# Sparse layer in another order, and wider products in the state-space mixer

## The reference

```python
h = rmsnorm(x, norm_mix_g)
proj = h @ w_in            # queries, shared key and value, index queries/key/weights, GLU pair
# index: relu(q_i . k_i) over 4 index heads, weighted and summed; causal; the top 128 keys of
#        each query are kept
# a_out: 8 heads of 64 attend over the kept keys (one key and value for all heads)
# b_out: u = a * sigmoid(g); causal depthwise convolution of 31 taps over 512 channels;
#        layer norm over the channels; silu
x = x + concatenate([a_out, b_out], -1) @ w_out
m = rmsnorm(mem, norm_mem_g)           # 256 memory tokens
kc, vc = m @ w_k_cross, m @ w_v_cross  # used by the cross attention that follows
...
# second block, first layer: a diagonal state-space mixer (S5) with complex states
lam_bar = exp(lam * dt); states = scan(lam_bar, B u); y = real(C states) + d * u
```

## Time and profile before

| | us |
|---|---|
| median of 3 runs | 2253.62 |
| lowest, highest | 2250.33, 2256.12 |
| the profiled execution, its own time | 2251.87 |
| its span (first to last instruction) | 2250.0 |
| TensorE busy in it | 2064.4 |
| VectorE busy | 1101.8 |
| ScalarE busy | 734.1 |
| GpSimd busy | 1066.6 |

### The profile page before, as it was taken

One profiled execution on the slowest core, in us unless ns is written; L12 is line 12 of the kernel. 1 busy time (PEld: TensorE's weight loads), 2 busy tenths in 40 slices (PEclk: granted clock), 3 DMA queues, 4 the chain that ended last, 5 costly groups with the idle time before them and its releaser, 6 DMA issues.

```text
span 2250.0 us, 30832 instructions
## 1 busy us (share of the span) xinstructions
PE 2064.4 (92%) x10090; PEld 1660.1 (74%) x10090; DVE 1101.8 (49%) x1843; ACT 734.1 (33%) x1216; POOL 1066.6 (47%) x607
## 2 busy tenths in 40 slices
PE   6879998978999989956899999999999999999997
PEld 5647766866787878735678888888877778888886
DVE  4798663255668676668534122132126743232232
ACT  4213054342322222435343222233224533222223
POOL 4455613633674744761255444456445515444442
PEclk9989987998999999988899999999998989999999
DMA  4314100313233333200133333334320003333332
GB/s 134 85 33 116 34 1 29 103 23 80 76 95 92 98 89 94 75 10 1 47 93 87 101 95 92 103 93 98 99 78 1 0 19 103 103 94 94 103 94 85
DMA packets 330830, 165.76 MB, mean 74 GB/s; under 512 B 21902, under 2 KB 329478, under 8 KB 330758
## 3 DMA queue, kind: packets, MB, share of 16 engines
q1 hardware_dynamic: 330016, 164.17, 25.9%
q10 hardware_dynamic: 742, 0.68, 0.2%
HBM read 162.48 MB, written 2.10 MB: 73 GB/s over the span
## 4 chain that ended last, share of the span: by engine, by line
PE 59%; issue 13%; DVE 8%; POOL 8%; POOLq 5%; DVEq 4%; ACT 2%; DMA 1%; SPq 0%; ACTq 0%
PE ACC L1248 16%; PE ACC L1254 16%; PE ACC L1249 16%; POOL WL L949 6%; POOLq L959 1%; PE O L1345 1%; PE ACC L1379 1%; PE O L1346 1%; PE O L1347 1%; POOLq L1098 1%; PE FOUR L1345 1%; POOLq L1086 1%; DVE CV L1777 1%; DVEq L1781 1%; DVEq L1847 1%
## 5 line engine op out<-in xcount | busy, mean ns | idle before, releaser
L949 POOL TENSOR_TENSOR WL<-RAW,WH 128x1024 fp32r<-128x1024 f32 x300 | 726.9, 2425 | 856.9 <-ACT WH L487 777.5
L1248 PE MATMUL ACC<-PH,WH 128*128 128x512 f32 x1248 | 495.7, 397 | 23.8 <-DVE DS L1787 11.1
L1249 PE MATMUL ACC<-PL,WH 128*128 128x512 f32 x1248 | 491.5, 394 | 0.0
L487 ACT ACTIVATE WH<-RAW 128x1024 fp32r<-128x1024 f32 x300 | 315.8, 1054 | 510.9 <-PE ACC L1254 461.1
L1248 PE MATMUL ACC<-QH,WH 128*128 128x512 f32 (+1 forms) x1136 | 433.6, 386 | 23.8 <-ACT WH L487 14.9
L1249 PE MATMUL ACC<-QL,WH 128*128 128x512 f32 (+1 forms) x1136 | 429.4, 382 | 0.0
L1254 PE MATMUL ACC<-PH,WL 128*128 128x512 f32 x1248 | 310.3, 391 | 0.0
L1248 PEld LDWEIGHTS ACC<-PH,WH 128*128 128x128 f32 x1248 | 238.2, 191 | 81.6 <-DVE DS L1787 12.4
L1254 PE MATMUL ACC<-QH,WL 128*128 128x512 f32 (+1 forms) x1136 | 269.7, 379 | 6.3 <-POOL WL L949 6.0
L1249 PEld LDWEIGHTS ACC<-PL,WH 128*128 128x128 f32 x1248 | 238.0, 191 | 48.9
L1248 PEld LDWEIGHTS ACC<-QH,WH 128*128 128x128 f32 x1136 | 218.0, 192 | 74.8 <-issue 15.9
(11 more groups left out here) (416 smaller groups left out, 2577.6 us busy)
## 6 DMA issues: line engine op xcount, KB each, us to landing
RAW<-in_mlp_w_dram SPq DMA_DIRECT2D x128, 512.0 KB, 3.8
RAW<-in_w_gate_dram SPq DMA_DIRECT2D x22, 512.0 KB, 3.7
RAW<-in_w_up_dram SPq DMA_DIRECT2D x22, 512.0 KB, 3.8
RAW<-in_w_in_dram SPq DMA_DIRECT2D x16, 512.0 KB, 3.8
RAW<-in_w_down_dram SPq DMA_DIRECT2D x16, 512.0 KB, 3.7
RAW<-in_ssm_w_glu_dram SPq DMA_DIRECT2D x16, 512.0 KB, 3.8
RAW<-in_w_kvf_dram SPq DMA_DIRECT2D x16, 512.0 KB, 4.0
RAW<-in_w_k_cross_dram SPq DMA_DIRECT2D x8, 512.0 KB, 3.7
```

The costliest lines, as they stand in the source:

```text
L487: act.activation(WH[:, s], RAW[:, s], ACT.Copy).then_inc(w_hi, 1)
L949: pool.tensor_tensor(WL[:, s], RAW[:, s], WH[:, s], ALU.subtract).then_inc(w_lo, 1)
L1248: pe.matmul(ACC[s][:, 0:n], WH[:, s, k, :], xh[:, k, :], start=(k == 0), stop=False)
L1249: pe.matmul(ACC[s][:, 0:n], WH[:, s, k, :], xl[:, k, :], start=False, stop=False)
```

## The change

The order of the sparse layer becomes: in (with rotations and index products between and inside its units), glu (with the memory's transposes; the rounds of the top 128 run beside it), memk, memv, then the sparse attention with the convolution among its tiles, then out in two halves. The rounds of the top 128 are written out, with other work of VectorE behind the first eleven. Taps 0 to 7 of VectorE come after them, one pair of the others behind each of 23 tiles. TensorE does three diagonal taps before the transposes of the tiles 0 to 10 and 12 to 22 (the last of each run fewer). The first two sets of diagonals are made between memk and memv, six in the attention. Out is split: outa multiplies the attention's half (four chunks of weights, 12 products), outb the branch's half; the layer norm and silu lie beside outa. At the start only the gain of the first norm is awaited ahead of x, and the broadcast of the scales of a norm stands inside unit 1. In the mixer a rotation is two products over 1024 columns and two sums of 512.

```diff
-ORDER = [("glu", 8), ("in", 8), ("memk", 8), ("memv", 8), ("out", 8), ("qc", 8), ("oc", 8)]
+ORDER = [("in", 8), ("glu", 8), ("memk", 8), ("memv", 8), ("outa", 8), ("outb", 8), ("qc", 8), ("oc", 8)]
...
         @block.scalar
+            rounded(5)
+            related(0)
+            rounded(6)
+            related(2)
+            related(4)
+            rounded(7)
...
+            memory(0)
+            gate(0)
+            rounded(11)
+            memory(2)
+            rounded(12)
+            memory(4)
+            gate(1)
+            rounded(13)
...
+            for j in range(8):
+                u = START["outa"] + j
+                round_weights(u + 1, 1 - j % 2, BCH)
+                if j == 2:
+                    standard_deviation("ln")
+                if j == 4:
+                    silu_branch()
...
         @block.gpsimd
+            with pool.Fori(0, 4) as i:
+                for s in range(2):
+                    remainder(START["memk"] + 2 * i + s, s)
+            diagonals(0)
+            diagonals(1)
+            with pool.Fori(0, 4) as i:
+                for s in range(2):
+                    remainder(START["memv"] + 2 * i + s, s)
+            remainder(START["outa"], 0, KC)
+            for j in range(2):
+                pool.wait_ge(u_hi, j + 1)
+                pool.tensor_tensor(UL[:, j, :], U[:, 2 + j, :], UH[:, j, :], ALU.subtract).then_inc(u_lo, 1)
...
         @block.tensor
+            unit(5, 1, PH, PL, between=lambda: relate(2))
+            rotate(4)
+            relate(4)
+            unit(6, 0, PH, PL, between=lambda: relate(6))
...
+            for j in range(1, 8):
+                unit(START["glu"] + j, j % 2, PH, PL)
+                if j < 5:
+                    memory(2 * j - 2)
...
+            def attend_sparse():
+                for t in range(3):
+                    scores("sparse", 0, 0, t)
+                for c in range(4):
+                    b = c % 2
+                    for t in range(8):
+                        n = 8 * c + t
+                        if t + 3 < 8:
+                            scores("sparse", c, b, t + 3)
+                        elif c < 3:
+                            scores("sparse", c + 1, 1 - b, t - 5)
+                        convolve_beside(n)
+                        turn("sparse", c, t)
+                        if t == 0 and c:
+                            values("sparse", c - 1, 1 - b, 1)
+                        if t == TB:
+                            values("sparse", c, b, 0)
+                        if n == CONV_END[1] + 3:
+                            branch_mean()
...
         @block.vector
+            for r in range(TOPK // 8):
                 for b in range(3):
                     dve.max(M8[:, b, :], SC[:, b, 0:(b + 2) * P])
                 dve.drain()
                 for b in range(3):
                     dve.match_replace(SC[:, b, 0:(b + 2) * P], M8[:, b, :], SC[:, b, 0:(b + 2) * P], TAKEN)
+                if r == 0:
+                    projected(7)
+                    roped(4)
+                    sines(5)
...
+                elif r == 3:
+                    roped(7)
+                    glu(0)
+                    glu_value(1)
+                    memory(0)
+                elif r == 4:
+                    glu_gate(1)
+                    memory(2)
...
+                        if n + 8 < CONVW:
+                            taps(n + 8, n + 9)
...
+            def turned(x, cos, sin, n):
+                both = [P, 2, 4, n]
+                dve.tensor_tensor(RTC[:, :, :, 0:n], x, cos[:, None].to_broadcast(both), ALU.mult)
+                return dve.tensor_tensor(RTS[:, :, :, 0:n], x, sin[:, None].to_broadcast(both), ALU.mult)
```

More of the change, by code:

```diff
@@ L46 @@
 TAKEN = -3.0e38
+CONV_END = (10, 22)
 LAG = 4
@@ L516, in _, with rounded @@
             act.activation(TRIR[:], TRI, ACT.Copy).then_inc(cst_r, 1)
-            round_weights(0, 0)
-            act.wait_ge(vec_c, 1)
+            act.wait_ge(vec_c, 2)
             act.activation(WCH[:], WC, ACT.Copy).then_inc(wc_hi, 1)
[L520 to L534, removed]
+            def rounded(u):
+                round_weights(u, u % 2)
             def memory(first):
@@ L1239, in _, with unit @@
         def _(pe):
-            def unit(u, s, xh, xl, n=T, kc=KC, chunks=None, norm=None):
+            def unit(u, s, xh, xl, n=T, kc=KC, chunks=None, between=None):
                 pe.wait_ge(w_hi, u + 1)
@@ L1279, in _ @@
                 mm.then_inc(x_t, 1)
[L1280 to L1289 removed]
+            pe.wait_ge(cst_in, 16)
@@ new lines, in _, with rotate @@
+            pe.wait_ge(gain_in, 16)
+            pe.transpose(ST[:, 0:KC], VROW[0:KC, 0, :], IDENT[0:KC, 0:KC]).then_inc(vec_t, 1)
+            for c in range(KC):
+                turn_x(c)
+            pe.wait_ge(vec_in, 16 * (len(VECTORS) - 1))
+            pe.wait_ge(vec_c, 1)
+            for t in range(3):
+                mm = pe.transpose(ST[:, t * P:t * P + ROWS[t]], VROW[0:ROWS[t], t, :], IDENT[0:ROWS[t], 0:ROWS[t]])
+            mm.then_inc(vec_t, 1)
+            def rotate(j):
+                rows = P if j not in (0, 3) else 64
+                pe.wait_ge(unit_out, START["in"] + j + 1)
+                if j >= 2:
+                    pe.wait_ge(rot_used, j - 1)
+                pe.matmul(TR[j % 2][0:rows, :], ROTM[0:rows, 0:rows], DS[0:rows, j, :], start=True, stop=True)\
+                  .then_inc(rot_done, 1)
@@ L1291, in memory, with relate @@
+            def relate(first):
+                for n in range(first, first + 2):
+                    qb, h = n // IDXH + 1, n % IDXH
+                    rows = slice(h % 2 * 64, h % 2 * 64 + 64)
+                    if n >= 2:
+                        pe.wait_ge(index_relu, n - 1)
+                    pe.matmul(S[n % 2][:, 0:(qb + 1) * P], DS[rows, 1 + h // 2, qb * P:(qb + 1) * P],
+                              KD[rows, 0, 0:(qb + 1) * P], start=True, stop=True).then_inc(index_mm, 1)
             def memory(first):
-                pe.wait_ge(mem_scaled, MB)
@@ new lines, in convolve_beside, with branch_mean @@
+            def convolve_beside(n):
+                first, last = CONV_END
+                if n <= first:
+                    convolve(3 * n, min(3 * n + 3, CONVW))
+                elif first + 1 < n <= last:
+                    m = CONVW + 3 * (n - first - 2)
+                    convolve(m, min(m + 3, 2 * CONVW))
+            def branch_mean():
+                pe.wait_ge(conv_done, 2)
+                pe.wait_ge(conv_pe, 2)
+                for c in range(BCH):
+                    mm = pe.matmul(ST[:], ONES, CV[c][:], start=(c == 0), stop=(c == BCH - 1))
+                mm.then_inc(mean_sum, 1)
@@ L1480, in normed @@
                 column_sums(norm)
-                unit(START[name] + 1, 1, xh, xl, norm=norm)
+                unit(START[name] + 1, 1, xh, xl, between=lambda: spread_scales(norm))
                 with pe.Fori(1, pairs) as i:
@@ L1922, in residual @@
+            for j in range(3, 8):
+                attended(j)
+            dve.drain()
             def residual(name, norm, gain, hi, lo, i):
```

657 lines of the change are left out of this document (392 added, 265 removed).

## The result

The changed kernel takes 2227.05 us (median of 4 runs, 2225.97 to 2232.6) against 2254.11 for the one before on the same chip: a ratio of 0.9881, with a 95% interval of 0.9869 to 0.9893. The profiled execution has a span of 2226.2 us, against 2250.0. The forecast was 2221, in a range of 2200 to 2245.

A forecast was written before the change was run, and what follows sets the result against it. TensorE was taken as busy 92% of the span, with VectorE's taps setting the in stage's end. Terms -6.7 - 27 + 6 - 5 + 9.5 - 7 = -30.2 took 2251.9 to 2221.7, say 2221, range 2200 to 2245.

The forecast's parts named there:

- The marks 35.1, 83, 141, 211: Forecast times in us: TensorE's unit 2, first MAX8 of the top 128, memory's first unit, first attention score.
- Start: Kernel's start: awaiting only the gain saves 4.7 us, moving the scales' broadcast 2; -6.7, bounds -4 and -8.
- In, index, glu: Unit 2 to memory's first unit: index and top 128 run beside other work, 7.4 us of waits; -27, bounds -34 and -9.
- rival D: In units: ScalarE's hand-written order makes TensorE wait about 3 us in each of 8; 2245, chance 0.07.
- Memory's units: Memory's units: two sets of diagonals in GpSimd's queue delay remainders and loads; +6, bounds +3 and +8.6.
- Attention: Sparse attention with convolution among its tiles: 129 us against 134.3; -5, bounds -15 and +26.
- so 1.46 + 0.35 + 2.0 = 3.8: VectorE's us per convolution tile: steady work, gaps, two taps; TensorE as much, so 4.0 for each of 23 tiles.
- Rival A: Attention tiles: TensorE, not VectorE, sets them at 3.55 us, and silus and squares hide; 2202, chance 0.20.
- B: Rival: taps queue behind GpSimd at 1.68 us, 2252, or the rounds delay all glu units, 2239; chance 0.15.
- C: Rival: every tile tap waits out a GpSimd instruction, about 2.8 us; slower, 2305, deciding from 1.87 a tap; chance 0.03.
- Out: Out units: roundings behind silus 5 us, broadcast 2, GpSimd's 3.0 a unit in outb 2.5; +9.5, bounds 0 and +15.
- Mixer: Mixer's sixteen rotations: 3.77 us each instead of 4.2, all on the chain; -7, bounds -2 and -12.

The follow-up runs named there:

- the diagonals kept: Changed kernel with GpSimd's six later sets of diagonals left out, TensorE's products reading what the first two sets left: 2222.14 us, 0.9864 of the kernel before.
- the run with all repairs: Changed kernel with five edits: early diagonals in glu, others on ScalarE, silus apart, UL and query copies in GpSimd's gaps, ML pairs a round earlier: 2203.52 us, 0.9784.

## Why the prediction was right, and where its terms were off

The time and the direction were right, 2227 for 2221, and so was the mechanism of the large term, -27 of -30.2; that of the attention was not. The marks 35.1, 83, 141, 211 came out as 34.2, 81.1, 139.1, 212.2, those behind them less well: the last O product at 337.8 and not 334, qc at 397.0 and not 388. The forecast is -30.2 and the spans differ by 23.8. The 6.4 us between them are a balance: memory's units, attention, out and mixer fell 9.1 short, and 2.6 came back in the start, in glu and behind qc.

- **Start**, -6.7, measured -7.6. Both parts came in: 5.9 for the 4.7 of the wait, 1.75 for the 2 of the broadcast.
- **In, index, glu**, -27, measured -27.4. The walk through the rounds gave the three waits to 0.3 us. That VectorE's taps had set the old stage is shown, with 15 us; rival D's waits in each in unit did not occur, as the clock of 1.00 and TensorE's 46.6 busy of 47.0 show.
- **Memory's units**, +6, measured +8.6, at the bound of 8.6. The idle 1.3 us a unit of GpSimd gave no cover: TensorE waited 7.4 for one remainder behind all four instructions. Idle time that lies in pieces between units does not take up a block of 8.
- **Attention**, -5, measured -2.5. Here the total is near by luck. The step "so 1.46 + 0.35 + 2.0 = 3.8" made VectorE the engine that sets the tiles, at 4.0 each, so 4 + 92 = 96 us to the 23rd tile; its transposes begin 96.1 behind the first score. But TensorE sets these tiles. With the diagonals kept the same mark is at 89.4, 3.6 a tile from the first, and the other 6.7 are one stall and the slow products behind it, which no term holds. "No cold clock, since TensorE no longer stands" failed twice: 0.57 behind the stall, and 0.51 in the first 10 us, behind the wait of 7.0 that the forecast itself had put ahead of the first score; that cost 2.7 us by the run with all repairs. What the stage is longer than forecast lies behind the 23rd tile, 29.6 us to the last O product where 17.6 + 4 + 5 were counted, and it is 29.5 with the diagonals kept too. Rival A had the right engine and nearly the right price (3.55), and missed the stall; B and C were wrong on the mean price of a tap. C's bound of 1.87 us a tap is a slip: 37/46 more than 1.0 is 1.80.
- **Out**, +9.5, measured +12.2, within +15. The queue behind the silus was right as a mechanism, 3.7 of it recovered by spreading them where 5 was forecast; outb's unit was 3.35 and not 3.0, some 2.8 over eight. Behind the wait of 2.8 the products run slowly (from 362 to 368 the clock is 0.73), behind the shorter ones they don't (1.00). Of the rest, the waits of 1.2 for the broadcast and 1.0 for a rounding at 370 can be seen; what else there is stays open.
- **Mixer**, -7, measured -5.7 (6.2 by the old rotations put back). Late chunks gain 0.95, as computed. The first rotation is no faster: from the first product to the first scan it is 22.4 us with the new rotations, 21.6 with the old ones put back and 22.5 in the kernel before, all beside GpSimd.

The 1.1 us between qc and the mixer were in no term. Code behind qc is the same in all kernels with the new rotations, and their time from qc's first product to the end varies from 1824 to 1832; why it does is open.

## What to carry to other kernels

When work is moved beside another engine's, a mean price tells what the moved instructions cost, not what the path does. Here 46 taps at 0.95 instead of 0.75 cost nothing as such, since TensorE set the tiles; one pair that met two GpSimd instructions in the shortest tile cost 6.7 us. So look for the place where the path has least to cover a block, and for the neighbours that share the contention. A block put into a queue is covered only by idle time of one piece and of its size; the same four instructions cost 7.4 us between the memory's remainders and nothing in glu. When work is taken from an engine to test whether it sets a stage, look at its clock as well, and ask the unchanged trace where that engine waited. And moving one waiting instruction ahead shifts the wait, unless all that stand in the same rhythm move.

## What the hardware showed unexpectedly

Two taps took 2.39 us each, where 0.74 is usual, across two GpSimd instructions of 1.91 and 2.36, and each ended 0.55 behind one of them, so each waited one out. ScalarE made the same diagonals in 92 copies of 128 columns, 28.8 us in all, and a tap beside them takes 0.76, against 0.75 with no diagonals made. And a stage from which 36 us of TensorE's products were taken kept its length while its granted clock fell from 0.89 to 0.71.
